# Turning tiles in the first out-projection, the keys stage and the last stage: type of the turn and place between products

## What is computed

```python
def _rmsnorm(x, g):
    y = xf * lax.rsqrt(jnp.mean(xf * xf, axis=-1, keepdims=True) + EPS)
    return (y * g).astype(x.dtype)

# layer A: gated short convolution
proj = rmsnorm(x, a_norm_pre) @ a_w_in            # 1024 -> 4096: b, c, h, z
y = silu(z) * b * conv3(c * h)
x = x + rmsnorm(y @ a_w_out, a_norm_post)         # the first out-projection
# keys, values, queries
k, v = (rmsnorm(x, kv_norm) @ w for w in (w_k, w_v))
q, z = split(rmsnorm(x, b_norm_pre) @ b_w_in)
# stick-breaking attention, 16 heads of 64
z_ = q @ k.T * scale
a = sigmoid(z_) * exp(sum of log_sigmoid(-z_) over the later keys)   # strictly causal
# the last stage holds the 8 streams' attention and the second out-projection
x = x + rmsnorm((silu(z) * (a @ v)) @ b_w_out, b_norm_post)
```

## Time and profile before

| what | value |
|---|---|
| time before, median of 3 runs | 2830.48 us (2828.51 to 2833.29) |
| the profiled execution's own time | 2826.52 us |
| its span, first to last instruction | 2824.9 us |
| granted TensorE clock over the span | 0.994 |
| TensorE busy | 2767.3 us, 98% of the span |
| VectorE, ScalarE, GpSimd busy | 58%, 47%, 41% |
| turns of the three stages that the change touches | 448 |

### The profile page before, as it was taken

How to read it: one execution, slowest core, us unless ns; L and a number is a source line. 1 busy time by engine, 2 the same in 40 slices (tenths; PEclk the granted TensorE clock), 3 DMA queues, 4 the chain that set the end, 5 groups by cost and what they waited for, 6 DMA issues and landing times. The chain is left out here.

```text
span 2824.9 us, 42046 instructions
## 1 busy us (share of the span) xinstructions
PE 2767.3 (98%) x14856; PEld 2420.5 (86%) x14856; DVE 1642.8 (58%) x2152; ACT 1316.6 (47%) x2733; POOL 1157.2 (41%) x1023
## 2 busy tenths in 40 slices
PE   7999999999999999999989999999999999989998
PEld 6999999999988888889978888888888888868886
DVE  5321232123244450102249999999999999998775
ACT  6000000000033341111148888888888888875443
POOL 3333333333220020002356877777777768651110
PEclk9999999999999999999999999999999999999999
DMA  5101110111064444424578676777777876767773
GB/s 159 39 25 37 38 38 22 38 38 38 9 210 134 126 155 151 173 102 153 166 216 267 197 244 198 236 215 216 221 223 208 251 203 208 220 187 210 231 225 105
DMA packets 280359, 433.33 MB, mean 153 GB/s; under 512 B 52578, under 2 KB 218594, under 8 KB 274180
## 3 DMA queue, kind: packets, MB, share of 16 engines
q1 hardware_dynamic: 269156, 391.41, 45.5%
q0 software_dynamic: 11040, 39.86, 4.8%
HBM read 307.40 MB, written 123.81 MB: 153 GB/s over the span
## 5 line engine op out<-in xcount | busy, mean ns | idle before, releaser
L1989 POOL TENSOR_TENSOR a_a<-a_a,a_prod 128x512 f32<-128x512 f32 (+3 forms) x640 | 661.9, 1052 | 272.0 <-DVE a_prod L1939 196.6
L1939 DVE TENSOR_TENSOR_SCAN a_prod<-a_keep,a_prod,a_restart 128x513 f32<-128x513 f32 x384 | 478.2, 1269 | 8.3 <-ACT a_keep L1883 7.5
L1882 ACT ACTIVATE a_a<-a_pz 128x512 f32<-128x512 f32 (+3 forms) x640 | 357.2, 559 | 70.9 <-PE a_pz L1807 46.6
L1949 DVE TENSOR_TENSOR a_atl<-a_pt,a_ath 128x512 fp32r<-128x512 f32 (+3 forms) x640 | 363.1, 599 | 32.3 <-ACT a_ath L1892 29.0
L1883 ACT ACTIVATE a_keep<-a_pz 128x512 f32<-128x512 f32 (+3 forms) x640 | 361.1, 565 | 0.0
L1892 ACT ACTIVATE a_ath<-a_pt 128x512 fp32r<-128x512 f32 (+3 forms) x640 | 332.8, 558 | 57.5 <-PE a_po L1821 34.1
L1832 PEld LDWEIGHTS a_pt<-a_ident,a_bits 128*128 128x128 f32 x2176 | 232.2, 141 | 51.7 <-DVE a_atl L1949 8.1
L279 POOL TENSOR_TENSOR w_wh<-w_raw,w_gain 128x1024 fp32r<-128x1024 f32 x22 | 42.6, 1936 | 534.6 <-PE v_pg L349 279.9
L1806 PE MATMUL a_pz<-a_kh,a_q 128*128 128x512 f32 (+3 forms) x640 | 247.6, 390 | 8.4 <-ACT a_keep L1883 5.8
L1819 PE MATMUL a_po<-a_ath,a_v 128*128 128x512 f32 (+3 forms) x640 | 250.1, 395 | 2.3 <-POOL a_v L2000 1.5
L1832 PE MATMUL a_pt<-a_ident,a_bits 128*128 128x128 f32 x2176 | 244.8, 242 | 7.1 <-DVE a_atl L1949 4.7
(11 more groups left out here) (234 smaller groups left out, 6151.5 us busy)
## 6 DMA issues: line engine op xcount, KB each, us to landing
a_x<-x_d SPq DMA_DIRECT2D x84, 896.0 KB, 6.7
a_x<-x_d SPq DMA_DIRECT2D x56, 832.0 KB, 6.0
a_kh<-kh_t SPq DMA_DIRECT2D x32, 512.0 KB, 7.1
a_kl<-kl_t SPq DMA_DIRECT2D x32, 512.0 KB, 9.1
w_raw<-in_a_w_in POOLq DMA_DIRECT2D x30, 512.0 KB, 4.9
x<-f_xn POOLq DMA_DIRECT2D x17, 512.0 KB, 6.4
g_y_in<-sz_t SPq DMA_DIRECT2D x17, 512.0 KB, 7.6
g_x<-x SPq DMA_DIRECT2D x17, 512.0 KB, 4.1
```

What stands on the lines that cost most here:

```text
L1882: act.activation(a[:, s, q, 0:w], pz[:, n % ZS, 0:w], ACT.Sigmoid, scale=SCALE)
L1939: dve.tensor_tensor_scan(prod[:, s, 0:w + 1][:, ::-1], keep[:, n % KS, 0:w + 1][:, ::-1], restart[:, 0:1].broadcast_to([P, w + 1]), prod[: ...
L1949: dve.tensor_tensor(atl[:, b % AS, c0:], pt[:, turn_slot(pr, hh, b), c0:], ath[:, b % AS, c0:].bitcast(F32), ALU.subtract).then_inc(at_spl ...
L1989: pool.tensor_tensor(part, part, prod[:, n % PS, after:after + w], ALU.mult).then_inc(weighted, 1)
```

## The change

Turns of the first out-projection, the keys stage and the last stage (all but `turn_out`) become float32r: the tile is read by a second name (`xs_bits`, `full_bits`, `k_bits`, `a_bits`), with `ident_r`, which VectorE now makes once at the program's start instead of at the attention stage's. They leave their rows and are put one by one between the matmuls of products:

- In `phase_out` the turns of tile u-2 no longer stand behind product u-1's last matmul but in product u, after the first and second matmul of kt 1 to 4 of its first half; the streams' tile takes tile 15's in kt 4 to 7 of its second half (begun before kt 4's products). ScalarE's `keep` of tile u-1 moves behind `tail` of tile u (`third_last`).
- In `phase_keys` a group's turns go into the second half of the next group's product.
- In `phase_finish`, steps 1 to 7, the weights' turns go into kt 5 to 6 of half(j,0,0); in steps 1 to 6 rounds 0 and 1 go into kt 4 to 7 of half(j,0,1), and rounds 2 and 3 from ahead of half(j,1,0) into its kt 0 to 1 and kt 3 to 4. Step 0 and the first 16 key turns keep their rows, as does line 1010, in the new type.

```diff
-        third(*at(k - 1))
+        if not third_last:
+            third(*at(k - 1))
...
+            dve.wait_ge(ident_loaded, 16)
+            dve.tensor_copy(ident_r[:, :], ident[:, :])
...
-def project(pe, out, w_h, w_l, x_h, x_l, a, n, kt0=0, kt1=KT):
+def project(pe, out, w_h, w_l, x_h, x_l, a, n, kt0=0, kt1=KT, between=nothing):
 
     for kt in range(kt0, kt1):
         r = slice(a, a + n)
         pe.matmul(out, w_h[:, kt, :], x_h[:, kt, r], start=(kt == 0), stop=False)
+        between()
         pe.matmul(out, w_h[:, kt, :], x_l[:, kt, r], start=False, stop=False)
+        between()
         mm = pe.matmul(out, w_l[:, kt, :], x_h[:, kt, r], start=False, stop=(kt == KT - 1))
     return mm
...
-            token_tiles(act, split_all, tail, keep, finish=False)
+            token_tiles(act, split_all, tail, keep, finish=False, third_last=True)
...
                 pe.matmul(o, yh[s][:, kt, :], border.wh(kt, r), start=(kt == 0), stop=False)
+                turn_one()
                 pe.matmul(o, yh[s][:, kt, :], border.wl(kt, r), start=False, stop=False)
+                turn_one()
                 return pe.matmul(o, yl[s][:, kt, :], border.wh(kt, r), start=False, stop=(kt == KT - 1))
 
             def multiply(j, s):
@@ -767,25 +777,30 @@
                     pe.wait_ge(normed[s], j)
                     for n in range(2):
                         for kt in range(KT):
+                            if n == 0 and kt == 1 and not (isinstance(j, int) and j == 0):
+                                begin_turn(j - 1, s)
+                            if n == 1 and kt == 4 and is_sample(j, s):
+                                begin_turn(*divmod(NT - 2, 2))
                             mm = products(s, n, kt)
-                            if is_sample(j, s) and n == 1 and kt == 4:
-                                turn_tile(*divmod(NT - 2, 2))
                         if is_sample(j, s) and n == 0:
                             mm.then_inc(g0_free, 1)
                 mm.then_inc(mm_done[s], 1)
 
-            def turn(j, s):
-                if not is_last_whole(j, s):
-                    turn_tile(j, s)
-
-            def turn_tile(j, s):
+            turns_left = collections.deque()
+
+            def begin_turn(j, s):
                 pe.wait_ge(scaled, 2 * j + s + 1)
                 pe.wait_ge(kept[s], j)
-                for kt in range(KT):
-                    mm = pe.transpose(pt[:, s, kt, :], xs[:, kt * P:(kt + 1) * P], ident[:, :])
-                mm.then_inc(turned[s], 1)
-
-            token_tiles(pe, multiply, turn, finish=False)
+                turns_left.extend((s, kt) for kt in range(KT))
+
+            def turn_one():
+                if turns_left:
+                    s, kt = turns_left.popleft()
+                    mm = pe.transpose(pt[:, s, kt, :].bitcast(F32R), xs_bits[:, kt * P:(kt + 1) * P], ident_r[:, :])
+                    if kt == KT - 1:
+                        mm.then_inc(turned[s], 1)
+
+            token_tiles(pe, multiply, nothing, finish=False)
...
-            def turn(c, g):
+            turns_left = collections.deque()
+
+            def begin_turn(c, g):
                 s, k = use(c, g)
                 pe.wait_ge(whole[s], k + 1)
                 wait_past(pe, rowed[s], k)
-                for i in range(GROUPS[g][1] // P):
-                    mm = pe.transpose(pt[:, s, i, :], full[:, s, i * P:(i + 1) * P], ident[:, :])
-                mm.then_inc(turned[s], 1)
-
-            def product(s, g):
+                turns_left.extend((s, i, GROUPS[g][1] // P) for i in range(GROUPS[g][1] // P))
+
+            def turn_one():
+                if turns_left:
+                    s, i, n = turns_left.popleft()
+                    mm = pe.transpose(pt[:, s, i, :].bitcast(F32R), full_bits[:, s, i * P:(i + 1) * P], ident_r[:, :])
+                    if i == n - 1:
+                        mm.then_inc(turned[s], 1)
+
+            def product(s, g, lagged=None):
                 a, n = GROUPS[g]
-                project(pe, pg[g][:, 0:n], wh[s], wl[s], xh, xl, a, n).then_inc(mm_done[s], 1)
+                project(pe, pg[g][:, 0:n], wh[s], wl[s], xh, xl, a, n, 0, KT // 2)
+                if lagged:
+                    begin_turn(*lagged)
+                project(pe, pg[g][:, 0:n], wh[s], wl[s], xh, xl, a, n, KT // 2, KT, turn_one)\
+                    .then_inc(mm_done[s], 1)
...
-                    mm = pe.transpose(half_pt[:, i, :], xs[:, kt * P:(kt + 1) * P], ident[:, :])
+                    mm = pe.transpose(half_pt[:, i, :].bitcast(F32R), xs_bits[:, kt * P:(kt + 1) * P], ident_r[:, :])
...
-                    product(c % 2, g)
-                    lagged = before(c, g)
-                    if lagged:
-                        turn(*lagged)
-            turn(KT - 1, NG - 1)
+                    product(c % 2, g, before(c, g))
+            begin_turn(KT - 1, NG - 1)
+            while turns_left:
+                turn_one()
...
+            def products(s, n, kt, between=nothing):
 
                 r = slice(n * W, (n + 1) * W)
                 o = ph[:, s, r]
                 pe.matmul(o, yh[s][:, kt, :], wh[:, kt, r], start=(kt == 0), stop=False)
+                between()
                 pe.matmul(o, yh[s][:, kt, :], wl[:, kt, r], start=False, stop=False)
-                return pe.matmul(o, yl[s][:, kt, :], wh[:, kt, r], start=False, stop=(kt == KT - 1))
-
-            def half(j, s, n):
+                between()
+                mm = pe.matmul(o, yl[s][:, kt, :], wh[:, kt, r], start=False, stop=(kt == KT - 1))
+                if kt < KT - 1:
+                    between()
+                return mm
+
+            def half(j, s, n, *turns):
+
+
+                turns, left = dict(turns), collections.deque()
+
+                def between():
+                    if left:
+                        left.popleft()()
+
                 if n == 0:
                     pe.wait_ge(y_lo[s], j + 1)
                     if not is_step(j, 0):
                         pe.wait_ge(normed, 2 * j + s - 1)
                 for kt in range(KT):
-                    mm = products(s, n, kt)
+                    if kt in turns:
+                        left.extend(turns[kt]())
+                    mm = products(s, n, kt, between)
                 if n == 1:
                     mm.then_inc(mm_done, 1)
-
-            def turn_keys(b, first, end):
-                if first == 0:
+                assert not left
+
+            def key_turns(b, r):
+
+                _, slot, kb, i0 = next(rounds(r, r + 1))
+                if r == 0:
                     pe.wait_ge(k_loaded, 16 * KB * (b + 1))
                     if not is_step(b, 0):
                         pe.wait_ge(at_ready, 2 * b)
-                for r, slot, kb, i0 in rounds(first, end):
-                    if r >= 2:
-                        pe.wait_ge(k_lo, NROUND * b + r - 1)
-                    for i in range(4):
-                        cols = slice((i0 + i) * P, (i0 + i + 1) * P)
-                        mm = pe.transpose(pka[:, slot, i, :], k_in[:, kb, cols], ident[:, :])
-                    mm.then_inc(k_turned, 1)
+                if r >= 2:
+                    pe.wait_ge(k_lo, NROUND * b + r - 1)
+
+                def one(i):
+                    cols = slice((i0 + i) * P, (i0 + i + 1) * P)
+                    mm = pe.transpose(pka[:, slot, i, :].bitcast(F32R), k_bits[:, kb, cols], ident_r[:, :])
+                    if i == 3:
+                        mm.then_inc(k_turned, 1)
+
+                return [lambda i=i: one(i) for i in range(4)]
+
+            def turn_keys(b, first, end):
+                for r in range(first, end):
+                    for one in key_turns(b, r):
+                        one()
...
+            def weight_turns(b, f):
+
+                if f == 0:
+                    if not is_step(b, 0):
+                        pe.wait_ge(o_read, 4 * b)
+                    else:
+                        pe.wait_ge(k_lo, NROUND)
+                pe.wait_ge(weighted, 2 * b + f + 1)
+
+                def one(kb, k0):
+                    mm = pe.transpose(pka[:, f, kb, :].bitcast(F32R), a_bits[:, f, k0:k0 + P], ident_r[:, :])
+                    if kb == NV - 1:
+                        mm.then_inc(a_turned, 1)
+
+                return [lambda kb=kb, k0=k0: one(kb, k0) for kb, k0 in enumerate(KEYS_AT)]
...
-                    half(j, 0, 0)
-                    turn_weights(j)
-                    half(j, 0, 1)
+                    half(j, 0, 0, (5, lambda: weight_turns(j, 0)), (6, lambda: weight_turns(j, 1)))
                     if not is_step(j, NB - 1):
-                        turn_keys(j + 1, 0, 2)
-                    weigh(j)
-                    if not is_step(j, NB - 1):
-                        turn_keys(j + 1, 2, NROUND)
-                    half(j, 1, 0)
+                        half(j, 0, 1, (4, lambda: key_turns(j + 1, 0)), (6, lambda: key_turns(j + 1, 1)))
+                        weigh(j)
```

(25 more changed lines are left out.)

38 lines of the change are left out of this document (20 added, 18 removed).

## The result

| | before | changed |
|---|---|---|
| median of six runs each, us | 2829.8 (2827.2 to 2833.29) | 2842.63 (2840.41 to 2844.44) |
| profiled execution, us; its span | 2826.52; 2824.9 | 2842.8; 2841.2 |

The ratio of the medians is 1.0044, 95% interval 1.0031 to 1.0057: slower by 0.44%, where 0.35% was forecast, and 12.8 us between the medians where the sum had 9.8.

What follows compares the result with a forecast made beforehand. TensorE, by its own queue, was taken to bound all three stages. Turn prices -0.1, identity's copy +0.1, border +1.8 and picking wait +8.0 made +9.8 us: 2840.3 us on the median 2830.48, range 2826 to 2846.

Steps and rivals of the forecast that it cites:

- the likeliest case: Whole kernel: the forecast of 2840.3 us, +0.35%, own range 2836 to 2846, chance 0.60 together with rival 4.
- A lone turn costs 0.111 us in either type: TensorE, three changed stages: a turn alone ahead of a product costs 0.111 us, against 0.110 now; 399 turns, +0.4 us.
- rival 1: TensorE: a lone turn is bound by its columns, 0.058 us, giving -20.7 us and 2819 us in all; chance 0.13.
- rival 2: TensorE: a lone turn costs 0.085 us as inside a row, giving 2829.9 us, no change; chance 0.13.
- In rows, 0.71 us for eight instead of 0.88: TensorE, rows that remain: eight float32r turns cost 0.71 us instead of 0.88; -0.5 us taken, -1.0 at most.
- Rival 4: Turns keep their float32 price ahead of any neighbour: the forecast plus 0.5 us; chance counted in the forecast's 0.60.
- The border, +1.8: Out-projection's end: tile 15's last turn and ScalarE's copy come later, so the barrier moves by +1.8 us (1.5 to 2.0).
- The wait before `turn_out`, 1.33 us in six steps, +8.0: Last stage, steps 1 to 6: TensorE waits 1.33 us a step for VectorE's picking; +8.0 us, bounds 6.6 to 9.0.
- Rival 3: Last stage: no wait before `turn_out`, VectorE's chain being shorter or TensorE later; 2832.3 us, no change; chance 0.14.
- Within the loop nothing comes late: Out-projection's loop: turns move by one kt (0.7 us), and VectorE's `xs` and ScalarE's copy have time to spare; no wait.
- Keys, 0: Keys stage: ScalarE's copy is there before the moved turns, 0 us; if late, under 0.5 us at each of 39 groups.
- Else in the last stage, 0 (up to +2.5): Last stage: round 0's turns wait for the weights' low parts, 0 us, or up to 0.4 us a step (+2.5).

Runs made afterwards that it cites:

- experiment 5: Changed kernel with key round 3's turns in the last stage begun at kt 5 of half(j,1,0) instead of kt 3; one execution, 2853.29 us.
- experiment 6: Changed kernel with key round 3's turns in the last stage begun at kt 2 of half(j,1,0) instead of kt 3; one execution, 2837.96 us.
- experiment 7: Changed kernel with only tile 15's eight turns back in a row, behind kt 4 of the out-projection's last tile; one execution, 2840.56 us.
- experiment 2: Changed kernel with all turns of the three stages float32 again, at their new places; 2841.61 us, ratio 1.0044 to the kernel before.
- experiment 1: Kernel before with the float32r type and the identity's copy at the start, turns in their old rows; 2820.57 us, ratio 0.9963 to the kernel before.
- Experiment 3: Changed kernel with VectorE picking ahead of rounds 2 and 3's low parts in last-stage steps 1 to 7; 2833.71 us, ratio 1.0012 to the kernel before.
- experiment 8: Changed kernel with the whole out-projection as before (rows, ScalarE's old order) but in float32r; 2836.9 us, ratio 1.0028 to the kernel before.

## Why the prediction was right, and where it was off

The sign, the likeliest case and the range held: 2842.63 us against 2840.3 and 2826 to 2846. By the prediction's own steps:

- **What bounds the kernel**: right. In steps 1 to 6 of the last stage each wait at `turn_out` came out as time in full (experiments 5 and 6), and at the border 1.7 us of it (experiment 7).
- **A lone turn costs 0.111 us in either type**: right, 0.110 to 0.113 (experiment 2). This ends rivals 1 (0.058) and 2 (0.085). The Trainium skill's rule (TensorE: Matmul & The Clock Gate, section "LDWEIGHTS (loading the stationary operand)", 107 ns for 128 columns) lies 3 to 6 ns below what was measured; no place in these traces went under 0.106.
- **In rows, 0.71 us for eight instead of 0.88**: right, 0.70 (experiment 1). Rival 4, that the type does nothing, is out; it would have given the same time here, as the prediction said.
- **The border, +1.8**: 1.71 by the profiles, 1.23 us of wait restored by experiment 7.
- **The wait before `turn_out`, 1.33 us in six steps, +8.0**: right in place, count and size. By starts, less the products around them, the two turns cost TensorE 1.55 us where they cost 0.22, 1.33 more; with the 0.11 us by which the first turn comes late, which the prediction didn't have, it is 1.44. The periods went from 32.25 to 33.68 us (33.6 forecast), 1.43 more, so all of it stands at `turn_out`. Experiment 3 takes 1.43 of a period away by VectorE's order alone and has the 32.25 us of before, with the turns still alone. Rival 3 is out.
- **"Within the loop nothing comes late": the step that failed.** The third tile's product waits 2.07 us for VectorE's low part in the changed kernel's profile, 0.35 to 0.46 at the least. The prediction reckoned with `xs` and the copies and not with the row as cover for the low part; and it took VectorE's lengths as fixed, though before, too, this very pass took 2.79 us at the third tile and 1.23 as the median of all sixteen.
- **Keys, 0**: +1.13 us. The 133 turns cost 0.0025 us more each than before, 0.3; the last one's wait is 0.58 us where it was 0.25, since a row no longer stands ahead of it, 0.3; of the remaining 0.5 the runs don't show the cause.
- **Else in the last stage, 0 (up to +2.5)**: +1.2 (9.76 less six times 1.43), about half in step 1 and half at the stage's opening. Step 1 has the wait for the weights' low parts that the prediction named and put at 0, at most 0.4 us a step. It comes in that step alone, for 0.4 us where the clock has fallen at the step's start (the profiles of changed and experiments 5 and 8) and for 1.9 to 2.0 where it hasn't (2, 3, 6 and 7), and never in the five profiles in which the stage's turns stand in rows. So the place was right and the size too small. The opening the prediction didn't look at: the score's first matmul waits 3.15 us for GpSimd's cast instead of 1.79 and starts 0.86 us later, of which 0.66 is left at the end of step 0. The changed kernel, then before:

```profile
2545.66 1.33 DVE L2577 TENSOR_TENSOR g_yl<-g_y_in,g_yh 128x1024 fp32r<-128x1024 f32 x1
2545.87 1.28 POOL L2257 CAST s_ktl<-s_knl 128x128 fp32r<-128x128 f32 x1
```

```profile
2539.49 0.29 POOL L2232 CAST s_ktl<-s_knl 128x128 fp32r<-128x128 f32 x1
2539.65 1.23 DVE L2516 TENSOR_TENSOR g_yl<-g_y_in,g_yh 128x1024 fp32r<-128x1024 f32 x1 [0.25 <-ACT g_yh L2420]
```

  The pattern is that of the third tile: with faster turns VectorE's pass comes 0.2 us ahead of the cast instead of behind it, and the cast takes 1 us longer. It does so in all ten profiles with float32r turns at this place, experiment 1's too; in experiment 2, with float32 turns, the cast has its 0.29 us and the wait is 1.54.
- **The sum**: 9.8 against 12.8 between the medians. The terms that were missing add up to 0.4 to 2.1 (third tile), 1.1 (keys), 1.2 (last stage) and 0.6 (six periods 0.1 longer than the wait), 3.3 to 5.0 us, against the 3.0 that lack, and step 1's wait can be 1.6 us longer still. That speaks for a third tile's wait near its lower end in most executions; it was not measured apart. The clock's fall (1.55) accounts for a part of the 16.3 us between the two profiles, and needn't be in the medians.

## What to carry to other kernels

The single-pass type made a 128-column turn cheaper only ahead of another turn (0.085 us instead of 0.110); between 512-column products it cost 0.110 to 0.113 us in either type, so here such turns belong in rows, with the type alone changed. That this price is the load of the next product's stationary side is the prediction's reading; the runs show the price and not the load. A row of turns is also cover: it hid what the next product waits for, and taking it apart lays bare every operand that comes in that last microsecond. When a step is moved later on one engine, read what stands behind it in the queues of the others; here one reordering on VectorE was worth 9 of the 12.8 us.

## What the hardware showed unexpectedly

- Where they overlapped, VectorE's and GpSimd's elementwise passes over SBUF held each other up: 1.23 to 2.84 us for an add, 0.29 to 1.28 for a cast, 1.89 to 2.90 for GpSimd's product, by which of the two started first, sometimes by 0.1 us. An edit that speeds one engine up can turn the order round.
- After 2.5 us without work, TensorE's granted clock fell about 1 us into the stage, for 3.4 us, in eight of twelve profiles of like kernels and not in the other four, at 1.55 us each time. At the start of the last stage's step 1 it fell in six of the twelve, and in kernels with turns alone that decided whether VectorE's lateness there showed as a wait of 2.0 us or of 0.4. Two waits in a row of 1.4 and 0.9 us, in a step otherwise full (experiment 5), were followed by such a fall in two of six steps.
